# Splitting a hybrid encoder step into a projection phase and one stream of attention, out-projection and MLP

## The reference, cut to what matters

```python
hn = rmsnorm(x, ln1_g) * (1.0 + sc1) + sh1          # sc, sh, g come from silu(c) @ w_ada + b_ada
z = hn @ w_in                                       # A: gated linear, B: RG-LRU, C: attention, D: short conv
...                                                 # q, k, v of group C: 4 heads of 64
z = einsum('bqhd,bkhd->bhqk', qb, k) * (SB_DH ** -0.5)     # stick breaking, blocks of 128 queries
mask = kpos[None, :] < qpos[:, None]
ls_neg = log_sigmoid(-z); ls_pos = ls_neg + z
lneg = where(mask, ls_neg, 0.0)
rest = cumsum(lneg, axis=3, reverse=True) - lneg
w = where(mask, exp(ls_pos + rest), 0.0)
o = einsum('bhqk,bkhd->bqhd', w, v)
...
mix = concatenate([o_a, o_b, o_c, o_d], axis=-1) @ w_out   # each o head-normed
x = x + g1 * mix
h2 = rmsnorm(x, ln2_g) * (1.0 + sc2) + sh2
x = x + g2 * (square(relu(h2 @ mlp_w1)) @ mlp_w2)          # D_FF = 4096
y = rmsnorm(x, final_g)
```

## Time and profile before

| what | us |
|---|---|
| median of 2 runs | 3273.94 (3269.42 to 3278.47) |
| profiled execution | 3273.41 |
| its span, first to last instruction | 3271.6 |
| PE busy | 2974.3 (91%) |
| DVE, ACT, POOL busy | 1512.7, 1241.1, 910.4 |

### The profile page before, as it was taken

The page is one execution under the profiler, slowest core; times in us unless marked ns, Lnnn a source line. Parts: engine busy times, 40 slices in busy tenths (PEclk is TensorE's granted clock), DMA queues, the critical chain, the costliest instruction groups (busy, mean ns, idle before and its releaser), DMA issues. The chain is left out here.

```text
span 3271.6 us, 43283 instructions
## 1 busy us (share of the span) xinstructions
PE 2974.3 (91%) x15985; PEld 2597.3 (79%) x15985; DVE 1512.7 (46%) x2336; ACT 1241.1 (38%) x1807; POOL 910.4 (28%) x472
## 2 busy tenths in 40 slices
PE   3798899889988898888957999999999999999997
PEld 1376667566756576666956999999999999999997
DVE  4506213731366206672025545546555456555555
ACT  4435434543455335453225222235322235322222
POOL 0142333033300333003004233246332345433330
PEclk9799989898988899897557999999999999999998
DMA  7232313031300332003523222221422212222220
GB/s 261 102 109 58 103 52 103 14 104 46 109 14 0 104 101 66 1 0 107 139 89 99 75 70 61 75 70 60 140 64 73 70 59 72 93 78 65 63 65 36
DMA packets 305775, 251.06 MB, mean 77 GB/s; under 512 B 10747, under 2 KB 268134, under 8 KB 305638
## 3 DMA queue, kind: packets, MB, share of 16 engines
q1 hardware_dynamic: 287238, 219.30, 22.3%
q10 hardware_dynamic: 18400, 29.89, 2.6%
HBM read 223.13 MB, written 21.70 MB: 75 GB/s over the span
## 5 line engine op out<-in xcount | busy, mean ns | idle before, releaser
L1659 DVE SCALAR_TENSOR_TENSOR xs<-op,modT,xs 128x352 f32<-128x352 f32 (+1 forms) x896 | 454.9, 528 | 201.4 <-PE op L1754 199.8
L1733 PE MATMUL hp<-h_hi,w1h 128*128 128x352 f32 x1536 | 497.6, 324 | 13.6 <-POOL h_lo L1483 13.6
L1752 PE MATMUL op<-g_hi,w2h 128*128 128x352 f32 x1536 | 501.0, 326 | 1.4 <-DVE xs L1659 1.1
L1734 PE MATMUL hp<-h_lo,w1h 128*128 128x352 f32 x1536 | 496.8, 323 | 0.0
L1735 PE MATMUL hp<-h_hi,w1l 128*128 128x352 f32 x1536 | 496.0, 323 | 0.0
L1753 PE MATMUL op<-g_lo,w2h 128*128 128x352 f32 x1536 | 495.2, 322 | 0.0
L1754 PE MATMUL op<-g_hi,w2l 128*128 128x352 f32 x1536 | 494.5, 322 | 0.0
L612 POOL TENSOR_TENSOR w_lo<-wraw,w_hi 128x1024 fp32r<-128x1024 f32 x122 | 296.9, 2434 | 463.8 <-ACT w_hi L648 454.7
L1472 POOL TENSOR_TENSOR w1l<-w1r,w1h 128x1024 fp32r<-128x1024 f32 x96 | 230.5, 2402 | 609.9 <-ACT w1h L1514 609.9
L1117 PE MATMUL zp<-hn_hi,w_hi 128*128 128x512 f32 x960 | 385.7, 402 | 3.8 <-ACT hn_hi L685 2.0
L1121 PE MATMUL zp<-hn_lo,w_hi 128*128 128x512 f32 x960 | 378.3, 394 | 2.5 <-POOL hn_lo L629 2.5
(11 more groups left out here) (256 smaller groups left out, 4147.9 us busy)
## 6 DMA issues: line engine op xcount, KB each, us to landing
wraw<-in_w_in_dram SPq DMA_DIRECT2D x96, 512.0 KB, 3.8
w1r<-in_mlp_w_dram SPq DMA_DIRECT2D x96, 512.0 KB, 4.1
w2r<-in_mlp_w_dram SPq DMA_DIRECT2D x96, 512.0 KB, 3.3
wraw<-in_w_out_dram SPq DMA_DIRECT2D x34, 512.0 KB, 4.1
wada<-in_w_ada_dram ACTq DMA_DIRECT2D x6, 2048.0 KB, 9.8
wada<-in_w_ada_dram SPq DMA_DIRECT2D x6, 2048.0 KB, 8.7
xs<-x_scratch SPq DMA_DIRECT2D x3, 2816.0 KB, 12.9
oT<-in_x_prompt_dram SPq DMA_DIRECT2D x4, 2048.0 KB, 7.6
```

The costliest lines, as they stand in the source:

```text
L1659: ins = dve.scalar_tensor_tensor(out=cols, in0=op[i % 4][:, a:e], scalar=modT[:, M_G2 + d, m:m + 1], in1=cols, op0=ALU.mult, op1=ALU.add)
L1733: pe.matmul(bank, w1h[ft][:, k, :], h_hi[:, k, cols], start=(k == 0), stop=False)
L1734: pe.matmul(bank, w1h[ft][:, k, :], h_lo[:, k, cols], start=False, stop=False)
L1752: pe.matmul(bank, wh, g_hi[odd][:, ft, cols], start=(ft == 0), stop=False)
```

## The change

`mixer_phase` keeps the projections and groups A, B and D with their norms. It writes xT, q, k and the six outputs of these groups to scratch tensors in DRAM (`x_scratch`, `q_scratch`, `k_scratch`, `o_scratch`), the past keys too. Tokens get a buffer of their own. Attention and out-projection leave it.

`tail_phase` replaces `mlp_phase`. It is fully unrolled and goes over blocks of 512 tokens, the last one with the sample's 64 in two groups of 288 columns. `walk` gives the order of its dense tiles: out-projection strips (`out`), norm sums (`nsum`), MLP-in strips (`hid`), MLP-out tiles (`prj`), final norm (`fsum`) and output turns (`yt`). All of them take turns on four PSUM banks `dn0` to `dn3` (`bank(u)` waits for the evacuation of tile u−4). Time is counted in slots of six matmuls; a `prj` tile is one slot, an `out` or `hid` strip four. Attention pairs are put on slots: the eight pairs of block 0 every 6 slots in a prologue that holds no dense tile, the other 76 every 11 slots, all before block 3's dense work. The steps of a pair follow at fixed offsets (SIG, SCAN, TURN, COPY, VALUES). There is one score buffer and one `left`, which the scan overwrites in place; the score uses the 64 rows of each head, with no padding. Weights are streamed once per block, four times in all. POOL now adds the squares and makes the low halves of h2.

```diff
-NORM_PAIRS = [2, 0, 6, 4]
-NORM_C = 3
+NORM_PAIRS = [2, 0, 6]
+NORMS_1 = 3
...
-    x1_dram = nc.dram_tensor("x1_scratch", (D_MODEL, N_TOK), F32, kind="Internal").ap()
+    x_v, o_v = scratch("x_scratch", D_MODEL, N_TOK), scratch("o_scratch", 6 * P, N_TOK)
+    q_v, k_v = scratch("q_scratch", GW, N_TOK), scratch("k_scratch", GW, N_TOK + PAST)
...
-        mlp_phase(nc, const, x1_v, mlp_w1, mlp_w2, y_prompt, y_sample)
+        tail_phase(nc, const, x_v, o_v, q_v, k_v, sbv_p, sbv_s, cache_sb_v, w_out, mlp_w1, mlp_w2, y_prompt, y_sample)
...
+    def groups(b):
+        return [(0, BLK)] if b < NB - 1 else [(0, HALF), (HALF, TMAX)]
...
+    SIG, SCAN, TURN, COPY, VALUES, FIN_OUT, FIN_TURN, FIN_COPY = 2, 5, (10, 12), (11, 13), (14, 15), 17, 19, 20
+    LEAD, PACE = 6, 11
+    before = sum(p.b == 0 for p in pairs)
+    beta = [LEAD * t for t in range(before)]
+    PRO = beta[-1] + FIN_COPY + 2
+    beta += [PRO + PACE * i for i in range(N_PAIRS - before)]
...
+        heads(0)
+        opening(0)
+        for b in range(NB):
+            for c in range(NC):
+                for ft in range(2):
+                    for g in range(len(groups(b))):
+                        hid(b, c, ft, g)
+                for d in range(KT if c else 0):
+                    for g in range(len(groups(b))):
+                        prj(b, c - 1, d, g)
+                    if c == 4 and b:
+                        yt(b - 1, d // 2, d % 2)
+                    if c == NC - 1 and d == 3 and b + 1 < NB:
+                        heads(b + 1)
+                if c == 2 and b:
+                    closing(b - 1)
+            if b + 1 < NB:
+                opening(b + 1)
+            for d in range(KT):
+                for g in range(len(groups(b))):
+                    prj(b, NC - 1, d, g)
...
+        dn = [ps(f"dn{i}") for i in range(4)]
+        sc, wt, ob = ps("sc", (P, 2, 512)), ps("wt"), ps("ob")
...
+            def scan(t):
+                p = pairs[t]
+                keep, x = left[0:p.rows, :, 0:p.w], taken[t % 2][0:p.rows, :, 0:p.w]
+                sums, upto = carry[0:p.rows, 2 * p.s:2 * p.s + 2], left[0:p.rows, :, p.w]
...
+                for j in range(2):
+                    ins = dve.tensor_tensor_scan(keep[:, j, ::-1], keep[:, j, ::-1], keep[:, j, ::-1],
+                                                 upto[:, j:j + 1], ALU.mult, ALU.min)
+                ins.then_inc(swept, 1)
+                dve.wait_ge(swept, t + 1)
+                dve.tensor_copy(sums, left[0:p.rows, :, 0])
+                dve.tensor_tensor(x, x, left[0:p.rows, :, 1:p.w + 1], ALU.mult).then_inc(w_ready, 1)
...
+                for j in range(2):
+                    rows = slice(HD * j, HD * j + HD)
+                    ins = pe.matmul(sc[0:p.rows, j, 0:p.w], q[rows, p.s * P:p.s * P + p.rows], k[rows, 0:p.w],
+                                    start=True, stop=not p.newest)
...
+            def bank(u):
+                if u >= 4:
+                    by, done = freed[u - 4]
+                    pe.wait_ge(evac[by], done)
+                return dn[u % 4]
```

More of the change, by code:

```diff
@@ new lines, in step, with square @@
+            def step(slot):
+                t = at_last.get(slot - FIN_COPY)
+                if t is not None:
+                    place(pairs[t].group)
+                for j in range(2):
+                    t = at.get(slot - COPY[j])
+                    if t is not None:
+                        copy(t, j)
+                t = at.get(slot - SIG)
+                if t is not None:
+                    sigmoids(t)
+            slots = Slots(step)
+            def square(kind, b, f):
+                k = norm_no[kind, b]
+                n = groups(b)[-1][1]
+                x = xs[b % 2][:, f, 0:n]
+                last = ("out", b, f) if kind == "second" else ("prj", b, NC - 1, f)
+                act.wait_ge(evac[PV], freed[tile_no[(*last, last_group(b))]][1])
+                if f == 0:
+                    wait(act, o_lo, KT * (b + 1) if kind == "second" else 0)
+                if f >= 3:
+                    act.wait_ge(n_acc, (KT - 1) * k + f - 2)
+                elif kind == "final":
+                    act.wait_ge(lo2, KT * (min(b + 1, NB - 1) + 1))
+                act.activation((st[f % 2] if f else nacc)[:, 0:n], x, ACT.Square).then_inc(n_sq, 1)
@@ new lines, in rows_of @@
+            def rows_of(b, i, v):
+                u, n = tile_no["yt", b, i, v], yt_no[b, i, v]
+                rows = token_tiles(b)[i]
+                act.wait_ge(d_full, u + 1)
+                wait(act, y_out[n % 2], 16 * (n // 2))
+                act.activation(yrow[n % 2][0:rows, :], dn[u % 4][0:rows, :], ACT.Copy).then_inc(evac[PA], 1)
+            for w in next_loads("start", 0):
+                weights_hi(w)
+            for i in range(6):
+                o_high(0, i)
+            slots.upto(PRO)
@@ new lines, in turn_out, with step @@
+            def turn_out(t):
+                p = pairs[t]
+                pe.wait_ge(osb_ok, p.group + 1)
+                wait(pe, wt_read, wt_no["fin", p.group])
+                for s in range(1 if p.sample else TPB):
+                    ins = pe.transpose(wt[:, s * p.rows:(s + 1) * p.rows], osb[0:p.rows, s * P:(s + 1) * P],
+                                       ident[0:p.rows, 0:p.rows])
+                ins.then_inc(wt_full, 1)
+            def step(slot):
+                for j in range(2):
+                    t = at.get(slot - VALUES[j])
+                    if t is not None:
+                        values(t, j)
+                t = at_last.get(slot - FIN_TURN)
+                if t is not None:
+                    turn_out(t)
+                for j in range(2):
+                    t = at.get(slot - TURN[j])
+                    if t is not None:
+                        turn(t, j)
+                t = at.get(slot)
+                if t is not None:
+                    score(t)
```

1363 lines of the change are left out of this document (722 added, 641 removed).

## The result

The changed kernel took 3361.76 us (median of 2 runs, 3356.3 to 3367.22) against 3273.94: a ratio of 1.0268 (95% interval 1.0174 to 1.0362). In a second series beside three of the experiments it took 3363.71 us, ratio 1.0281 (1.0241 to 1.0321). So it is slower, by 88 us. The forecast was 3240, and 3361.76 lies just above the upper end of its range, 3360.

What follows compares the result with a forecast made beforehand. It took PE, busy 91%, as the bound, with losses at key-block borders and low clock. Terms 1023 + 79 + 1625 + 295 + 92 + 38 + 12 + 5 + 19 + 20 + 30 gave 3238 of span, 3240 us; range 3130 to 3360.

Steps and rivals of the forecast that it cites:

- The 1728 positions: Dense out-projection and MLP work: 192 and 1536 positions at 940 ns each, 1625 us in all.
- rival of narrow matmuls bound by weight loads: Matmuls of 288 columns take up to 158.7 ns instead of 132, +92 us, so 3332; chance 0.04.
- Phase one: Blocks before the tail, without their own attention and out-projection, follow at some 193 us and end at about 1023 us.
- The eight first pairs: First block's attention ahead of all dense work: 31 us for loads, 33.5 for the single-buffer loop, 19 after; +79.
- the scan chain: DVE's scans, copy and product before bank-emptying adds: 6.5 us against 3.8 covered, about 17 pairs, 38 us with turns.
- the openings: Each block's first MLP chunk, where norm steps precede the adds: 26 + 3 × 22 = 92 us, including low clock.
- my bad end: Upper case of the scan-chain term: 80 us if the chain takes some 10 us.
- the end: Close of the kernel after the dense work: 30 us, by the 28.6 of before.
- the smaller terms: ScalarE held before openings 12 us, weight halves there 5, norm sums and output turns 19, final norms 20.
- Attention on PE: 76 threaded pairs cost their PE time, 50 full × 4.33 and 26 smaller × 3.04: 295 us, no score overlap.
- DVE paces the stream: Slower rival: a 9 us chain delays 38 of 76 pairs, 198 us in place of 38, so 3400; chance 0.13.
- The stalls hide: Faster rival: terms from the chain on mostly vanish, down to about 3090, middle 3165; chance 0.32.

Runs made afterwards that it cites:

- e1: Changed kernel with POOL's low halves of the streamed weights cut to one eighth of their columns (stale, computation left out): 3218.48 us, ratio 0.9855.
- e5: Changed kernel with the score of both heads made over all 128 partitions instead of 64 per head (output not attention's): 3384.9 us, ratio 1.0362.
- e7: Changed kernel with the 76 threaded pairs' slots chosen so scans stand in MLP-in strips or out-projection, never among MLP-out tiles: 3298.99 us, ratio 1.0086.
- e12: Changed kernel with each of POOL's low halves of a weight in four pieces of 256 columns, nothing left out: 3284.48 us, ratio 1.0069.

## Why the prediction was wrong

What bounds the kernel, and the pace. The 1728 positions took what was forecast: 225.5 and 132 ns a matmul (the stretch 3100 to 3150 has 379 records in 50 us, 131.9 ns). That falsifies the rival of narrow matmuls bound by weight loads.

Phase one ended at 1027.9, forecast 1023. Its blocks follow each other at 194.6 us (first turns at 507.76 and 702.33), forecast 193. The eight first pairs took until 1115.0, 87 us for 79: 34 until the last strips had landed (31), and the loop at the low clock.

**The step that failed is the scan chain**, and in it the count: "each of the about 17 pairs that fall wholly into projection tiles". The chain's length was right. From carry copy to the end of the product, DVE's records have 54 full chains in the stream, 4.0 to 10.0 us long, with a mean of 6.60; I had put 6.5. But after 41 of the 76 pairs the next DVE instruction is an add that empties a dense bank (32 in MLP-out tiles, nine in out-projection strips). I had counted only chains that begin early enough in the eight tiles to hold four banks, and left out those at the end of the strips, which reach into the tiles: ScalarE runs ahead, and DVE comes to the first adds late. With 41 in place of 17 the same working gives 41 × (6.6 − 3.8) = 115 less what smaller pairs save; measured were 83 us in 30 waits outside the openings (27 longer than a microsecond), against 38, with 80 as my bad end. The 80 stood for a chain of 10 us, which did not come; it was reached by the count.

**A term was missing**: the clock. I charged 2.5 us for each opening and none in the stream. Dense matmuls outside the openings came 108 us slower than 225.5 and 132 ns. Laid beside the granted clock of the same trace, 42 of them fall to matmuls at the low clock or at its edges, as after 1294.84. Another 36 are the 0.10 us behind each piece of attention (five pieces a pair: the score, two turns, two products with the values; 0.085 in the gap from 1303.90 to 1304.21, behind a turn), and 12 the 0.03 us ahead of each. Some 19 are left: 15 of a pace a little over 225.5 ns, and 4 at the last matmul before a stall. In e1, where most of these stalls are gone, the slower part is 36 us smaller, 33 of it at the low clock.

Together: 5 + 8 + (83 − 38) + 42 of clock + 19 of pace is 119. Attention, the openings and the end below give back 5 + 3 + 2, and the smaller terms add 4. That is 113 of the 3354.4 − 3238 = 116 us that the span is above the sum.

The openings: 69 us of gaps and 20 of slower matmuls in four of them, 89, forecast 92. The MLP's start was a good nearest row. One of them, in the timeline of all engines:

```profile
2304.52 2.67 POOL L1495 TENSOR_TENSOR t_st<-t_st 128x512 f32<-128x512 f32 x2
...
2307.34 2.04 PE L1950 MATMUL t_dn<-t_st,ones 128*128 128x512 f32 x2 [6.34 <-POOL t_st L1495]
...
2310.80 0.69 DVE L1802 TENSOR_TENSOR t_rt<-t_xs,t_rms 128x512 f32<-128x512 f32 x1 [8.45 <-ACT t_rms L1665]
...
2326.83 0.79 PE L1970 MATMUL t_dn<-t_g_hi,t_w2h 128*128 128x512 f32 x1 [10.55 <-DVE t_xs L1784]
```

POOL's last add of squares ends at 2307.19, the sum and the rms take 3.6 us, DVE starts its eight steps at 2310.80, and PE waits 10.55 us for the adds behind them, as the prediction's order had it.

Attention on PE: 242 us on its own rows (values 105.6, score 73.0, turns 49.3, mask 11.6, turned outputs 2.6) and some 48 behind and ahead of them, 290 for a forecast of 295. The forecast had miscounted the pairs: 54 of the 76 are full and 22 smaller, not 50 and 26. At its own prices that would be 301. Within it the score was cheaper than I took it, by the overlap that I had ruled out from the earlier trace rows. That was a misreading. The view puts the four matmuls in one row, and I divided 0.73 by four. In the single records of the same trace they start in pairs 7 ns apart, at 281.726 and 281.733 and at 282.046 and 282.053, just as the score's do after the change. The overlap could be seen before. Without it the kernel would be 21 to 26 us slower still, as e5 is. The smaller terms (ScalarE's waits, output turns, norm sums, final norms) came to some 60 in place of 56, and the end to 28.4 for 30.

The rivals: "DVE paces the stream" is what happened, at a weaker price. Its count was nearly right, 38 of the 76 pairs for 41, and its chain of 9 us was not: that length came in 5 of 54. The outcome is the rival's count with the forecast's chain. It had 0.13, and passed 3340 by itself only at 7.4; what took the kernel beyond were these waits and the clock together, and the clock I had named there without a price. That the time lies so near the upper end of the range is no merit of the working: the count and the clock were not in it. "The stalls hide" was false.

Where the gain went: the attention's PE time fell from 495 us in its stretches (84 pairs and their norms) to 290 (76 pairs), as planned. It was given back as waits for adds held behind scans (83), as low clock after them, as the openings (89), and as a first block of attention that nothing overlaps (87, where before it was 89.9 with its out-projection).

## What to carry to other kernels

Before work of one engine is threaded into a stream, count in program order how many of its pieces stand directly ahead of an instruction that the bounding engine waits for; and price the low clock after each such wait beside the wait. Where an operation of POOL can hold DVE, its length counts: four pieces of 256 columns in place of one of 1024 gave 69 to 79 us for an edit of one instruction, and 37 to 43 where the order had been mended first. A view that merges rows can hide that instructions run side by side: look at their single starts before a sum is built on them. And put the long chain where another engine frees PE's banks, if it is held: e7 won 64 to 65 us so, in part because the scans also met POOL less there.

## What the runs showed of the hardware

A POOL operation with SBUF operands holds not only DVE operations with two SBUF inputs but a copy of two columns too: 1.04 us for 0.17, ending 0.02 us after POOL's; over 48 such copies the mean was 0.88. The adds with one input in PSUM kept their 0.75 us beside POOL (mean 746 ns in the changed kernel, 747 in e1). With POOL's operations a quarter as long (e12), 512-column scans fell from 1995 to 1560 ns and the copies to 0.43 us, and with them nearly gone (e1) the scans to 1328.

Two score matmuls with 64 partitions each, one per half, took 1.06 us in four instructions, where the same columns over 128 partitions took 1.72. The instructions of the two halves start 7 ns apart. Put between dense matmuls, the score of a full pair cost the stream 0.46 us less so.

In the changed kernel's stream every stall of PE of 3.0 us or more outside the openings was followed by some 3 to 6 us at the low clock, matmuls of 512 columns every 0.43 us; of the shorter ones of 2.2 to 3.0 us some were (2.26 us before 1353.24) and some were not (2.26 us before 2053.31). Outside the openings the low clock cost some 42 us beside the 83 us of waits for the adds.
